# A decoder layer in split fp32: in w_up, one 512-column matmul takes the high and the low half of the activations together

## The reference

```python
h = rms_norm(x, norm_ffn_g[i])
u = causal_dwconv(h @ w_up[i], ffn_conv_w[i])      # w_up: 2048 x 11264, 3 taps
u_g, u_v = jnp.split(u, 2, axis=-1)
x = x + (jax.nn.silu(u_g) * u_v) @ w_down[i]       # w_down: 5632 x 2048
```

## Time and profile before

| | us |
|---|---|
| median of 3 runs | 1655.7 (1655.46 to 1656.33) |
| span of the profiled execution | 1654.6 |
| PE busy | 1639.9, 12970 matmuls |
| PE weight loads busy | 1605.2, 12970 loads |
| VectorE busy | 1028.1 |
| ScalarE busy | 750.2 |
| DMA | 55% of 16 engines, 178 GB/s |

### The profile page before, as it was taken

One profiled execution on the slowest core, in us unless ns is written; L12 is line 12 of the kernel. 1 busy time (PEld: TensorE's weight loads), 2 busy tenths in 40 slices (PEclk: granted clock), 3 DMA queues, 4 the chain that ended last, 5 costly groups with the idle time before them and its releaser, 6 DMA issues.

```text
span 1654.6 us, 31828 instructions
## 1 busy us (share of the span) xinstructions
PE 1639.9 (99%) x12970; PEld 1605.2 (97%) x12970; DVE 1028.1 (62%) x1203; ACT 750.2 (45%) x869; POOL 31.4 (2%) x53
## 2 busy tenths in 40 slices
PE   7999999999999999999999999999999999999998
PEld 7989998999999999999999999999999999999987
DVE  6599655655566546566576666664446666675754
ACT  5444444434555444444544454443334445444453
POOL 5000000000000000000000000000000000000000
PEclk9999999999999999999999999999999999999999
DMA  7555544555555565555555556555555555555554
GB/s 234 180 178 179 167 152 153 166 166 155 178 163 163 179 185 170 192 179 191 179 173 174 190 184 192 179 185 184 180 188 168 178 190 179 194 177 188 177 182 149
DMA packets 154282, 294.42 MB, mean 178 GB/s; under 512 B 9383, under 2 KB 11795, under 8 KB 154192
## 3 DMA queue, kind: packets, MB, share of 16 engines
q1 hardware_dynamic: 153648, 292.85, 55.1%
q0 software_dynamic: 512, 0.27, 0.1%
q10 hardware_dynamic: 32, 0.01, 0.0%
HBM read 291.00 MB, written 2.10 MB: 177 GB/s over the span
## 4 chain that ended last, share of the span: by engine, by line
PE 99%; DMA 0%; DVE 0%; ACT 0%; SPq 0%; issue 0%; DVEq 0%; ACTq 0%
PE acc L449 29%; PE acc L450 29%; PE acc L451 28%; PE acc L474 3%; PE acc L476 3%; PE acc L475 3%; PE fb L554 1%; DMA xtok<-in_x 0%; PE fa L491 0%; PE fa L508 0%; PE fa L568 0%; PE fb L587 0%; ACT junk L795 0%; PE fb L577 0%; PE fb L508 0%; PE fb L588 0%
## 5 line engine op out<-in xcount | busy, mean ns | idle before, releaser
L1045 DVE TENSOR_TENSOR w_lo<-raw,w_hi 128x1024 fp32r<-128x1024 f32 x550 | 669.6, 1223 | 583.0 <-ACT w_hi L778 582.9
L778 ACT CAST w_hi<-raw 128x1024 fp32r<-128x1024 f32 x550 | 571.0, 1047 | 679.4 <-PE acc L451 604.0
L449 PE MATMUL acc<-h_hi,w_hi 128*128 128x256 f32 x2704 | 769.2, 284 | 3.1 <-DVE h_lo L1051 3.1
L451 PE MATMUL acc<-h_hi,w_lo 128*128 128x256 f32 x2704 | 765.8, 283 | 0.0
L450 PE MATMUL acc<-h_lo,w_hi 128*128 128x256 f32 x2704 | 765.8, 283 | 0.0
L449 PEld LDWEIGHTS acc<-h_hi,w_hi 128*128 128x128 f32 x2704 | 519.7, 192 | 3.7 <-issue 3.3
L450 PEld LDWEIGHTS acc<-h_lo,w_hi 128*128 128x128 f32 x2704 | 519.6, 192 | 0.1
L451 PEld LDWEIGHTS acc<-h_hi,w_lo 128*128 128x128 f32 x2704 | 519.6, 192 | 0.0
L450 PE MATMUL acc<-f_lo,w_hi 128*128 128x256 f32 x704 | 199.2, 283 | 0.0
L451 PE MATMUL acc<-f_hi,w_lo 128*128 128x256 f32 x704 | 198.9, 282 | 0.0
L449 PE MATMUL acc<-f_hi,w_hi 128*128 128x256 f32 x704 | 197.3, 280 | 0.0
(11 more groups left out here) (261 smaller groups left out, 1307.8 us busy)
## 6 DMA issues: line engine op xcount, KB each, us to landing
raw<-in_w_up SPq DMA_DIRECT2D x176, 512.0 KB, 3.5
raw<-in_w_gate SPq DMA_DIRECT2D x96, 512.0 KB, 3.8
raw<-in_w_in SPq DMA_DIRECT2D x90, 512.0 KB, 3.5
raw<-in_w_down SPq DMA_DIRECT2D x88, 512.0 KB, 4.3
raw<-in_w_out SPq DMA_DIRECT2D x32, 512.0 KB, 4.3
raw<-in_w_ple_gate SPq DMA_DIRECT2D x32, 512.0 KB, 4.3
raw<-in_w_moba_out SPq DMA_DIRECT2D x16, 512.0 KB, 3.5
raw<-in_w_conv_out SPq DMA_DIRECT2D x8, 512.0 KB, 3.5
```

The lines of the kernel that those rows point to most:

```text
L449: nc.tensor.matmul(dst, stat_hi, mov_hi, start=first, stop=False, skip_group_check=True)
L451: return nc.tensor.matmul(dst, stat_lo, mov_hi, start=False, stop=last, skip_group_check=True)
L778: A.copy(w_hi[:, c % RING, :], raw[:, c % RING, :]).then_inc(chunk_high, 1)
L1045: V.tensor_tensor(w_lo[:, c % RING, :], raw[:, c % RING, :], w_hi[:, c % RING, :].bitcast(F32), ALU.subtract).then_inc(chunk_split, 1)
```

## The change

The high and low halves of each split activation become one tensor, `[P, tiles, 2, S]`: for each feature tile the 256 high values are followed by the 256 low ones. In w_up the matmul with the high half of the weights takes these 512 columns at once, into one whole PSUM bank: columns 0 to 255 receive hi x hi, columns 256 to 511 hi x lo. The third product (lo x hi) stays a matmul of 256 columns and adds into columns 256 to 511. An accumulator of w_up is thereby four banks wide, `wide[0]` banks 0 to 3 and `wide[1]` banks 4 to 7; `acc`, `fa` and `fb` are views of the same eight banks. ScalarE copies the columns 256 to 511 of the four banks out (`low_part`), VectorE adds the columns 0 to 255 to them, which now releases the accumulator, and multiplies by `rB` in a second instruction. `taps0` waits for that (`up_scaled`) and comes behind the rounding of one more chunk. The sums for `rB` move from `fa` to `fb`, and TensorE waits for the copy of `rB` before the first value group.

All other matmuls keep their shapes; they read and write the halves through views (`h_hi`, `h_lo` and so on).

```diff
-    h_hi = new("h_hi", [P, KD, S], F32R)
-    h_lo = new("h_lo", [P, KD, S], F32R)
+    h_both = new("h_both", [P, KD, 2, S], F32R)
...
-    acc = [nc.alloc_psum_tensor(f"acc{i}", [P, QD, S], F32) for i in range(2)]
-    fa = nc.alloc_psum_tensor("fa", [P, 2, 512], F32)
-    fb = nc.alloc_psum_tensor("fb", [P, 2, 512], F32)
+    psum = nc.alloc_psum_tensor("psum", [P, 8, 512], F32)
+    acc = [psum[:, b:b + 2, :].rearrange("p b (j s) -> p (b j) s", j=2) for b in (0, 6)]
+    fa = psum[:, 2:4, :]
+    fb = psum[:, 4:6, :]
+    wide = [psum[:, QD * i:QD * i + QD, :] for i in range(2)]
...
+    def halves(t):
+        return t[:, :, 0, :], t[:, :, 1, :]
+
+    h_hi, h_lo = halves(h_both)
...
+        def wide_chunk(c, part, kt, first, last, i, step):
+
+            pe.wait_ge(chunk_split, i * step + (c + 1))
+            for k in range(2):
+                for j in range(QD):
+                    w = slice(k * W + j * P, k * W + (j + 1) * P)
+                    nc.tensor.matmul(wide[part][:, j, :], w_hi[:, c % RING, w], h_both[:, kt + k, :, :].rearrange("p h s -> p (h s)"),
+                                     start=first and k == 0, stop=False, skip_group_check=True)
+                    mm = nc.tensor.matmul(wide[part][:, j, S:2 * S], w_lo[:, c % RING, w], h_both[:, kt + k, 0, :],
+                                          start=False, stop=last and k == 1, skip_group_check=True)
+            mm.then_inc(chunk_used, 1)
...
                     pe.wait_ge(taken[part], i + group0 // 2)
+                    if part == 1 and u_first:
+                        pe.wait_ge(rB_taken, 1)
                     for j in range(8):
                         if part == 0 and u_first and j % 2 == 0:
                             pe.wait_ge(unit_split, U_X1 + j // 2 + 1)
-                        feature_chunk(c0 + 8 * part + j, part, h_hi, h_lo, 2 * j, j == 0, j == 7, i, 16)
+                        wide_chunk(c0 + 8 * part + j, part, 2 * j, j == 0, j == 7, i, 16)
...
+        def low_part(k, dst, i, used):
+
+            act.wait_ge(chunk_used, used)
+            earlier()
+            A.copy(dst[:, :, 2:], wide[k][:, :, S:2 * S]).then_inc(low_sums, 1)
+
+        def taps0(src, dst, col, i, need):
+
+            act.wait_ge(up_scaled, need)
...
-                taps0(1, upv, cv, FT + 4 * pair0, i, i + (group0 // 2 + 1))
-                for k in range(20, 23):
+                low_part(1, upv, i, i * 16 + (c0 + 16))
+                high(c0 + 20, i, 16)
+                taps0(upv, cv, FT + 4 * pair0, i, i * 2 + (2 * pair0 + 2))
+                for k in range(21, 23):
                     high(c0 + k, i, 16)
...
+                def scaled(k, dst, i, count, groups):
+
+                    dve.wait_ge(low_sums, count)
+                    V.tensor_tensor(dst[:, :, 2:], wide[k][:, :, 0:S], dst[:, :, 2:], ALU.add).then_inc(taken[k], 1)
+                    dve.wait_ge(taken[k], groups)
+                    V.tensor_tensor(dst[:, :, 2:], dst[:, :, 2:], quad(rB[:]), ALU.mult).then_inc(up_scaled, 1)
...
                 earlier()
-                dve.wait_ge(chunk_used, i * 16 + (c0 + 16))
-                V.tensor_tensor(upv[:, :, 2:], acc[1][:], quad(rB[:]), ALU.mult).then_inc(taken[1], 1)
+                scaled(1, upv, i, i * 2 + (2 * pair0 + 2), i + (group0 // 2 + 1))
                 split(c0 + 20, i, 16)
```

More of the change, by code:

```diff
@@ L199, in trunk @@
     gt = ar("gt", [P, QD, S], 86)
[L200 to L203, removed]
+    o_both = ar("o_both", [P, QD, 2, S], 68, F32R)
+    c_both = ar("c_both", [P, HEADS, 2, S], 56, F32R)
     sc = ar("sc", [P, 2, 3 * P], 82)
     pT = ar("pT", [P, 2, 3 * P], 78)
[L206 to L209, removed]
+    m_both = ar("m_both", [P, KD, 2, S], 32, F32R)
+    p_both = ar("p_both", [P, 2, 2, S], 64, F32R)
     ptok = ar("ptok", [P, TT, PLE], 76)
@@ L270, in trunk @@
     cv_ready, folded = sem("cv_ready"), sem("folded")
+    rB_taken, low_sums, up_scaled = sem("rB_taken"), sem("low_sums"), sem("up_scaled")
     def unit_dst(u):
@@ L446, in _, with products, feature_chunk @@
     def _(pe):
[L447 to L453, removed]
+        def products(dst, stat_hi, stat_lo, mov, first, last):
+            nc.tensor.matmul(dst, stat_hi, mov[:, 0, :], start=first, stop=False, skip_group_check=True)
+            nc.tensor.matmul(dst, stat_hi, mov[:, 1, :], start=False, stop=False, skip_group_check=True)
+            return nc.tensor.matmul(dst, stat_lo, mov[:, 0, :], start=False, stop=last, skip_group_check=True)
+        def feature_chunk(c, s, a_both, kt, first, last, i=None, step=0):
             pe.wait_ge(chunk_split, c + 1 if i is None else i * step + (c + 1))
@@ L604, in _ @@
                     pe.wait_ge(unit_split, U_H + c + 1)
-                feature_chunk(c, s, h_hi, h_lo, 2 * j, first, last)
+                feature_chunk(c, s, h_both, 2 * j, first, last)
             elif name in ("gv", "mv"):
@@ L612, in _ @@
                     w = slice(k * P, (k + 1) * P)
-                    mm = products(acc[s][:, 0, :], w_hi[:, c % RING, w], w_lo[:, c % RING, w], h_hi[:, 8 * j + k, :],
-                                  h_lo[:, 8 * j + k, :], first and k == 0, last and k == 7)
+                    mm = products(acc[s][:, 0, :], w_hi[:, c % RING, w], w_lo[:, c % RING, w], h_both[:, 8 * j + k, :, :],
+                                  first and k == 0, last and k == 7)
                 mm.then_inc(chunk_used, 1)
@@ L726, in down @@
                             pe.wait_ge(unit_split, u0 + j // 2 + 1)
-                        feature_chunk(c0 + half * n + j, half, f_hi, f_lo, 2 * j, j == 0, j == n - 1, i, 2 * n)
+                        feature_chunk(c0 + half * n + j, half, f_both, 2 * j, j == 0, j == n - 1, i, 2 * n)
         up(UP1, PAIRS1, NG_UP1, True)
@@ L955, in up @@
                 highs[0] = i * 16 + (c0 + 12)
-                taps0(0, upg, cg, 4 * pair0, i, i + (group0 // 2 + 1))
-                for k in range(12, 15):
+                low_part(0, upg, i, i * 16 + (c0 + 8))
+                high(c0 + 12, i, 16)
+                taps0(upg, cg, 4 * pair0, i, i * 2 + (2 * pair0 + 1))
+                for k in range(13, 15):
                     high(c0 + k, i, 16)
```

42 lines of the change are left out of this document (22 added, 20 removed).

## The result

| | before | after |
|---|---|---|
| median, us | 1656.0 (1655.5 to 1657.4) | 1647.5 (1646.4 to 1651.4) |
| span of the profiled execution, us | 1654.6 | 1646.0 |
| matmuls | 12970 | 11562 |
| VectorE busy, us | 1028.1 | 1056.2 |
| ScalarE busy, us | 750.2 | 776.6 |

The ratio after to before is 0.9945 (95% interval 0.9931 to 0.9960). The change makes the kernel 8.5 us faster, where 18.8 us were forecast. At 1647.5 us it lies 1.5 us above the stated range, and 0.2 us from the time of rival A.

The account below looks back on a forecast made before the run. TensorE, fed without a break, was taken to bound the kernel: span 1654.6 - 18.8 (matmuls; all else nothing) = 1635.8 us, with 1.1 us to the median 1636.9. Range 1632 to 1646 us, the forecast's own 1635.5 to 1638.5.

Parts of the forecast that it names:

- rival A: w_up: alternating makes every 512-column matmul take 0.234 us as in w_ple; 8.4 us gained, 1647.3 us; chance 0.10.
- Matmuls: w_up: each of 1408 pairs falls from 0.3600 to 0.3466 us by one load's fixed 0.0134 us; 18.8 us gained.
- B: w_up: weights loaded early behind 512 columns bring the next matmul sooner, 0.343 us a pair; 23.5 us gained, 1632.2 us; chance 0.07.
- the bounds of the unknown cost: w_up's alternating stream: a pair takes between 0.3366 us (32.9 us gained) and 0.36 us (nothing gained).
- Leaving the accumulators: Exit of each w_up group: ScalarE's added copy (1.03 us) and VectorE's second operation (1.23 us) run beside TensorE; cost nothing.
- Supply: Weights for w_up: transfers, rounding and subtraction keep up with a chunk shortened from 2.880 to 2.773 us; no cost.
- TensorE's waits: The new wait for rB's copy before the first value group, and the release of the four-bank accumulators; cost nothing.
- new strides: Split activations with halves side by side: writes go to rows 512 apart, matmuls still read contiguous columns; cost nothing.
- Rival C: Behind w_up groups: the longer exit starves TensorE, for instance 2.2 us per pair of groups, 1661 us; chance 0.05.
- D: w_up: a 512-column matmul between short ones takes as long as the two it replaces, 0.24 us; 1655.7 us; chance 0.04.

Follow-up runs that it names:

- g2: The changed kernel with its layout, four-bank accumulators and longer exit, but three 256-column matmuls per w_up pair as before the change; 1656.1 us, ratio 0.9994.
- e1: The changed kernel with each w_up chunk's eight 512-column matmuls issued first, then its eight 256-column ones; 1644.8 us, ratio 0.9919.
- e7: The changed kernel with each w_up chunk's matmuls grouped by kind, the order of kinds turned round in every second chunk; 1639.8 us, ratio 0.9899.
- e4: The changed kernel with the working area (p, m, a, o, c, f) moved up by 32 bytes per partition, to a multiple of 64 bytes; 1642.4 us.
- b4: The kernel before with h_hi moved by 32 bytes and the working area 256 bytes above a multiple of 512 from the weight ring; 1635.5 us.
- g1: The kernel of e4 run once more, unchanged; 1643.2 us.
- b1: The kernel before with only h_hi, and all behind it, moved up by 64 bytes per partition against the weight ring; 1632.4 us, ratio 0.9853.
- f2: The kernel of e7 with h moved by 32 bytes and the working area at offset 64 bytes; 1611.1 us, ratio 0.9718.
- b2: The kernel of b1 with the working area also 64 bytes above a multiple of 512 from the weight ring; 1634.3 us, ratio 0.9868.
- k1: The kernel of e7 with h and the working area both at offset 64 bytes; 1622.0 us, ratio 0.9786.
- k2: The kernel before with the offsets of f2 (h at 32, working area at 64 bytes) and nothing else; 1621.2 us, ratio 0.9781.

## Why the prediction was wrong

**The step that failed** is *Matmuls*: 1408 x 0.0134 = 18.8 us. The w_up stages gained 1408 x 0.0067 = 9.4 us. The direction and the place were right. The size rested on the sentence that both kinds cost their columns "and 0.0133 us more, once for each instruction". Two rows that agree had been read as a law. They agree only for operands at offset 0 in a stream of one kind; g2 shows that nothing but the long matmul is behind the gain. e1 and e7 show that the alternation takes the missing part: with the same matmuls grouped, w_up gains 15.2 and 16.9 us. e4 to b4 show that the excess is no property of the instruction.

**What had been on the table.** The rows for it stood in the document: w_ple's 0.234 us and the 0.24 us behind a change of kind. I took the steady values "since the deviations die out after a few instructions on both sides". That was the argument to distrust: in the new stream every instruction is the first behind a change. Taken together, the two seams come close: 0.235 us on the mean behind the long ones of the earlier trace rows and 0.117 behind the short ones of the earlier trace rows make 0.352 us a pair, against the measured 0.3533. The prediction gave them to two rivals, A and B, and never added them. Rival A came out at 1647.3 us against the measured 1647.5, with a chance of 0.10, but partly by luck: it had 0.234 us for the long matmul, from a stage that doesn't alternate, and 0.120 for the short one; the long one was dearer (0.236) and the short one cheaper (0.117), and the two misses nearly cancel. The high end of 1646 us cut off two thirds of A, where the bounds of the unknown cost (0.3366 to 0.36 us per pair) had asked for up to 1655.7.

**The rule of the Trainium skill** (TensorE: Matmul & The Clock Gate, "Back-to-back issue gap": columns over 2.4 GHz and about 2.5 ns, which the section gives for an isolated matmul) doesn't fit these streams either. No long fp32r stretch at the full clock came below 6.7 ns over its columns, and in streams of one kind the excess went up to 21 ns. The estimate of 3.5 us gained that was made from it lies 5 us below the measured 8.5, the forecast 10 us above.

**Leaving the accumulators** was right to a few tenths of a microsecond. Let G be the first matmul behind the value group, now 1434.41; chunk 23 is first multiplied at 1454.57:

```profile
1434.41 0.28 PE L456 MATMUL psum<-f_both,w_hi 128*128 128x256 f32 x1
...
1454.57 0.28 PE L456 MATMUL psum<-f_both,w_hi 128*128 128x256 f32 x1
```

VectorE's timeline (answering to the earlier trace rows) is:

```profile
1437.04 1.23 DVE L1423 TENSOR_TENSOR upv<-psum,upv 128x1024 f32<-128x1024 f32 x1
1438.30 1.23 DVE L1425 TENSOR_TENSOR upv<-upv,rB 128x1024 f32<-128x1024 f32 x1
1439.45 1.22 DVE L1076 TENSOR_TENSOR w_lo<-raw,w_hi 128x1024 fp32r<-128x1024 f32 x1
1441.60 1.67 DVE L1431 SCALAR_TENSOR_TENSOR cv<-upv,fw,cv 128x256 f32<-128x256 f32 x4 [0.93 <-ACT cv L977]
...
1447.16 1.22 DVE L1467 TENSOR_TENSOR full<-cg,cv 128x1024 f32<-128x1024 f32 x1
1450.53 1.23 DVE L1076 TENSOR_TENSOR w_lo<-raw,w_hi 128x1024 fp32r<-128x1024 f32 x1 [2.15 <-ACT w_hi L799]
```

The addition starts at G+2.6 (forecast G+2.6), the split of chunk 20 at G+5.0 (G+5.2), the convolution at G+7.2 (G+7.0), `full` at G+12.8 (G+12.6), and the split of chunk 23 ends at G+17.4 (G+17.2). TensorE wants that chunk at G+20.2 here, 2.8 us later; the forecast's G+19.4 holds for chunks of w_up, while the chunks behind this last group belong to w_down, at 2.88 us each. The copy that makes room, and the taps behind the product, on ScalarE:

```profile
1435.69 1.02 ACT L970 COPY upv<-psum 128x1024 f32<-128x1024 f32 x1
...
1439.73 1.71 ACT L977 ACTIVATE cv<-upv,fw 128x256 f32<-128x256 f32 x4 [1.19 <-DVE upv L1425]
```

**Supply, TensorE's waits and new strides** were put at nothing, and g2 bears that out as a whole (0.9994). Rival C (starvation) is out, as TensorE has no wait there; B (a gain by early loads) and D (no gain) are out by the pair's 0.3533 us. B's observation was real, though: short matmuls behind long ones take 0.117 us on the mean. What they give back is less than the long ones lose.

**What stays open.** Why alternating makes the long matmul take 0.236 us, and by what rule a stretch settles at 0.1133 or 0.1178 us. That weight loads and streamed columns get into each other's way is a guess: no run took the loads away. The work of the other engines does not look like the cause, since in the first w_down stage of the kernel before every stretch of 54 matmuls has the same 0.1200 us, while VectorE is busy from 42% (1120 to 1140 us) to 75% (1080 to 1100 us). Shown is only that order, place and the stream before each decide on some nanoseconds, and that the one kernel that was profiled twice repeated its distances (e4, g1).

## What to carry to other kernels

In a kernel bound by back-to-back matmuls, measure the start-to-start distance of each stage against columns over the clock, and treat the excess as something that order and placement can change: here 64 bytes in one allocation gained 24 us (b1), and merging 1408 matmuls 8.5. If long and short matmuls have to share a stream, try them in groups, with the order turned round from chunk to chunk: that brought the gain in w_up from 9.4 to 16.9 us here. And when a new pattern is priced from the steady state of its parts, look at the few odd distances at the seams in both directions and add them up, since the new pattern is all seams.

## What the runs showed of the hardware

- At the full clock an fp32r matmul with its weight load cost from 0.0067 us (w_down in f2) to 0.0133 us (before) over its columns in long stretches of 256 columns, and 0.0133 to 0.0207 us at 512 (w_ple the most). With the activations at offset 0 the 256-column matmuls took longest (0.1200 us, as at 96) and the 512-column ones of the last stage shortest (0.2267 us).
- Alternating 512- and 256-column matmuls on the same operands took 0.3533 us a pair; grouped by eight 0.3492, and with the order turned round in every second chunk 0.3480, where the steady distances add up to 0.3467.
- The working area at one offset (64 bytes) ran w_out at 0.1178 us in b2 and k1 and at 0.1133 in f2 and k2; what differed was the offset of h, read in the stages before.
- Thirty-two matmuls of 1 and 64 columns, 3.3 us of work, came together with a clock at 1.2 GHz, at them or just behind, in 13 of 20 profiled executions and not in the other seven; in the one of the changed kernel it cost about 1.6 us.
